# Three small layouts of a hybrid attention/mLSTM block: made by transfers in place of TensorE operations

## The reference

```python
def rmsnorm(x, g):
    y = x32 * lax.rsqrt(jnp.mean(x32 * x32, axis=-1, keepdims=True) + EPS)
    return (y * g.astype(jnp.float32)).astype(x.dtype)

# window_sink_attention: CHUNK = 64, a query chunk sees its own and the previous chunk
v_band = jnp.concatenate([shift_chunks(v, j) for j in (1, 0)], axis=2)      # 128 keys per query chunk
out = jnp.einsum('bnkgqs,bnskd->bnqkgd', probs, v_band)

# mlstm_chunkwise: state carried from chunk to chunk
m_new = jnp.maximum(f_l + m_st, m_l)
a = jnp.exp(f_l + m_st - m_new)
c_new = a[..., None, None] * c_st + e[..., None, None] * c_l
num = s_qk @ v + w_inter[..., None] * jnp.einsum('bhntk,bhnkv->bhntv', q, c_prev)

# reference
h = rmsnorm(x, norm1_g[l])
x = x + hybrid_mixer(h, w_in[l], ...)       # z = h @ w_in + b_in; attention | mLSTM; norms; @ w_out
h = rmsnorm(x, norm2_g[l])
x = x + conv_ffn(h, w_up[l], ...)           # 1024 -> 2*2816 -> 1024
return rmsnorm(x, final_g)
```

## Time and profile before

| what | value |
|---|---|
| median of 3 runs | 1001.22 us |
| profiled execution, its own time | 1000.0 us |
| its span, first to last instruction | 998.3 us |
| TensorE busy (matmuls) | 990.3 us, 99% |
| VectorE, ScalarE, GpSimd busy | 741.0, 508.1, 54.1 us |
| granted TensorE clock, mean | 0.999 |
| TensorE in the chain that ended last | 97% |

### The profile page before, as it was taken

The page is one execution under the profiler, slowest core; times in us unless marked ns, Lnnn a source line. Parts: engine busy times, 40 slices in busy tenths (PEclk is TensorE's granted clock), DMA queues, the critical chain, the costliest instruction groups (busy, mean ns, idle before and its releaser), DMA issues.

```text
span 998.3 us, 12909 instructions
## 1 busy us (share of the span) xinstructions
PE 990.3 (99%) x4725; PEld 812.0 (81%) x4725; DVE 741.0 (74%) x1155; ACT 508.1 (51%) x979; POOL 54.1 (5%) x53
## 2 busy tenths in 40 slices
PE   9999999999999999999999999999999999999997
PEld 7788887877888888888888888888888888888886
DVE  4573667866655669997777777777776879996796
ACT  5663556575633236754445445545445534444573
POOL 1000323311300000000000000000000000000000
PEclk9999999999999999999999999999999999999999
DMA  9528565223722242342232223223223999045104
GB/s 343 190 75 244 169 210 174 81 84 143 281 85 85 85 127 84 106 126 65 84 94 77 64 96 95 64 85 105 63 85 122 393 345 320 1 123 192 34 1 169
DMA packets 93256, 133.98 MB, mean 134 GB/s; under 512 B 5884, under 2 KB 56188, under 8 KB 93192
## 3 DMA queue, kind: packets, MB, share of 16 engines
q1 hardware_dynamic: 92664, 132.72, 39.9%
q10 hardware_dynamic: 432, 0.42, 0.1%
q0 software_dynamic: 96, 0.00, 0.1%
HBM read 104.75 MB, written 28.35 MB: 133 GB/s over the span
## 4 chain that ended last, share of the span: by engine, by line
PE 97%; DVE 1%; issue 1%; POOL 0%; ACT 0%; ACTq 0%; POOLq 0%
PE pz L2086 8%; PE pz L2369 8%; PE pz L2370 8%; PE pz L2371 8%; PE pd L2369 6%; PE pd L2370 6%; PE pd L2371 6%; PE pd L2393 4%; PE pd L2390 4%; PE pd L2392 4%; PE pz L2390 3%; PE pz L2393 3%; PE pz L2392 3%; PE pd L2272 3%; PE pd L2274 3%; PE pd L2273 3%
## 5 line engine op out<-in xcount | busy, mean ns | idle before, releaser
L1133 ACT ACTIVATE ws_hi<-raw 128x512 fp32r<-128x512 f32 x88 | 52.9, 626 | 102.8 <-PE pz L2371 47.3
L2369 PE MATMUL pz<-ht_hi,ws_hi 128*128 128x512 f32 x240 | 93.5, 390 | 0.0
L2371 PE MATMUL pz<-ht_hi,ws_lo 128*128 128x512 f32 x240 | 93.4, 389 | 0.0
L2370 PE MATMUL pz<-ht_lo,ws_hi 128*128 128x512 f32 x240 | 93.4, 389 | 0.0
L2369 PE MATMUL pd<-ht_hi,ws_hi 128*128 128x512 f32 x200 | 77.9, 389 | 0.0
L2371 PE MATMUL pd<-ht_hi,ws_lo 128*128 128x512 f32 x200 | 77.8, 389 | 0.0
L2370 PE MATMUL pd<-ht_lo,ws_hi 128*128 128x512 f32 x200 | 77.8, 389 | 0.0
L1836 DVE SCALAR_TENSOR_TENSOR gate<-u,vec,gate 128x1023 f32<-128x1023 f32 (+1 forms) x44 | 56.5, 1284 | 19.4 <-ACT gate L1175 18.6
L1806 DVE TENSOR_TENSOR ws_lo<-raw,ws_hi 128x512 fp32r<-128x512 f32 x88 | 58.6, 687 | 0.7 <-ACT ws_hi L1133 0.7
L1836 DVE SCALAR_TENSOR_TENSOR lift<-u,vec,lift 128x1023 f32<-128x1023 f32 (+1 forms) x44 | 56.3, 1279 | 0.1
L1208 ACT ACTIVATE d_hi<-a 128x512 fp32r<-128x512 f32 x44 | 27.7, 631 | 53.6 <-PE pd L2393 25.0
(11 more groups left out here) (311 smaller groups left out, 2562.9 us busy)
## 6 DMA issues: line engine op xcount, KB each, us to landing
raw<-in_w_up SPq DMA_DIRECT2D x48, 512.0 KB, 5.0
b<-in_w_down SPq DMA_DIRECT2D x49, 256.0 KB, 6.8
act_rows<-gate SPq DMA_DIRECT2D x22, 512.0 KB, 2.6
a<-act_rows SPq DMA_DIRECT2D x44, 256.0 KB, 4.6
w_raw<-in_w_wide SPq DMA_DIRECT2D x16, 512.0 KB, 3.4
x_turned<-in_x_t SPq DMA_DIRECT2D x8, 512.0 KB, 9.1
x_in<-in_x SPq DMA_DIRECT2D x8, 512.0 KB, 12.8
wo_hi_rows<-wo_new_hi SPq DMA_DIRECT2D x8, 512.0 KB, 5.1
```

Of the source, the lines that this page charges most:

```text
L1133: nc.scalar.activation(ws_hi[m][:, :, :], summand(p, i), ACT.Copy).then_inc(s["ws_hi_made"], 1)
L2369: mm(dst, wh[:, k, :], xh[:, k, :], start=begins and k == 0, stop=False, skip_group_check=not begins)
L2370: mm(dst, wh[:, k, :], xl[:, k, :], start=False, stop=False, skip_group_check=not begins)
L2371: ins = mm(dst, wl[:, k, :], xh[:, k, :], start=False, stop=k == KH - 1, skip_group_check=not begins)
```

## The change

Three things, all in the first 150 us of the program.

1. `x` is loaded in tiles of consecutive rows, so ScalarE's sums and the inverted roots come out as `rstd_tok` at once (token 128i + p at partition p, column i). SyncE stores that tile in order of tokens, now element by element: 1024 pieces of 4 bytes in place of 128 pieces of 32 bytes. The eight transposes and the copy are gone.
2. `carry` is filled by four transfers from the rows in memory, 64 x 8 elements of 4 bytes each, behind each head's `q_inter` in `spread_rows`. The two matmuls, `pair_rows` (a memset and a select on GpSimd) and the copy are gone; `rows_spread` counts 12 transfers, not 8.
3. `att_vb` is filled by two transfers that move the halves of `att_va`'s partitions, behind `load_tile(11)`. Seven transposes and two ScalarE copies are gone; `attend(2)` waits for the two transfers.

```diff
             def load_x(i):
-                sp.dma_start(x_in[:, i, :], x_d[i:S:NT, :]).then_inc(x_loaded[i // 4], 16)
+                sp.dma_start(x_in[:, i, :], x_d[i * P:(i + 1) * P, :]).then_inc(x_loaded[i // 4], 16)
...
             sp.wait_ge(s["x_rstd"], 1)
-            sp.dma_start(rstd_d.rearrange("(p i) -> p i", i=NT), rstd[:, :]).then_inc(s["rstd_stored"], 16)
+            sp.dma_start(rstd_d.rearrange("(i p) -> p i", p=P), rstd_tok[:, :],
+                         allow_slow_non_contiguous=True).then_inc(s["rstd_stored"], 16)
...
                     sp.dma_start(q_inter[(h % 2) * 64:(h % 2) * 64 + 64, h // 2, :],
                                  inter_d[h, :].partition_broadcast(64)).then_inc(s["rows_spread"], 16)
+                    sp.dma_start(carry[(h % 2) * 64:(h % 2) * 64 + 64, h // 2, :],
+                                 inter_d[h, P - 1:S:P].partition_broadcast(64),
+                                 allow_slow_non_contiguous=True).then_inc(s["rows_spread"], 16)
...
                 if n == 8:
                     spread_rows()
+                if n == 11:
+                    sp.wait_ge(s["att_v_made"], 1)
+                    for a in range(2):
+                        sp.dma_start(att_vb[a * CHUNK:(a + 1) * CHUNK, :, :],
+                                     att_va[(1 - a) * CHUNK:(2 - a) * CHUNK, a:a + NT - 1, :])\
+                          .then_inc(s["att_v_moved"], 16)
...
             def decay_keep(i):
                 if i == 0:
-                    pool.wait_ge(s["rows_spread"], 16 * 8)
+                    pool.wait_ge(s["rows_spread"], 16 * 12)
...
-                for c, dst in enumerate((att_va[:, 0:4, :], att_va[:, 4:8, :], att_vb[:, 0:4, :], att_vb[:, 4:7, :])):
+                for c, dst in enumerate((att_va[:, 0:4, :], att_va[:, 4:8, :])):
...
-            nc.vector.reciprocal(rstd[:, :], root[:, :]).then_inc(s["x_rstd"], 1)
+            nc.vector.reciprocal(rstd_tok[:, :], root[:, :]).then_inc(s["x_rstd"], 1)
...
-                dve.wait_ge(s["gates_turned"], 2)
-                nc.vector.tensor_copy(rstd_tok[:, :], bank[5][:, 2 * NT:3 * NT])
-                nc.vector.tensor_copy(carry[:, :, :], bank[5][:, 0:2 * NT].rearrange("p (r i) -> p r i", r=2))
+                dve.wait_ge(s["gates_turned"], 1)
...
             ins.then_inc(s["gates_turned"], 1)
-            pe.wait_ge(s["inter_made"], 1)
-            for r in range(2):
-                ins = mm(bank[5][:, r * NT:(r + 1) * NT], pair_rows[0:ML_HEADS, r, :], row_c[0:ML_HEADS, P - 1:S:P],
-                         start=True, stop=True)
-            pe.wait_ge(s["rstd_spread"], 16)
-            for i in range(NT):
-                ins = nc.tensor.transpose(bank[5][:, 2 * NT + i:2 * NT + i + 1], rstd_row[0:1, i * P:(i + 1) * P],
-                                          ident[0:1, 0:1])
-            ins.then_inc(s["gates_turned"], 1)
             z_block(7)
...
-                for n in range(2 * NT - 1):
-                    k0 = n * P if n < NT else CHUNK + (n - NT) * P
-                    ins = nc.tensor.transpose(bank[4 + n // 4][:, (n % 4) * P:(n % 4 + 1) * P], z[:, AV, k0:k0 + P],
-                                              ident[:, :])
+                for n in range(NT):
+                    ins = nc.tensor.transpose(bank[4 + n // 4][:, (n % 4) * P:(n % 4 + 1) * P],
+                                              z[:, AV, n * P:(n + 1) * P], ident[:, :])
...
                 c = n % 2 * 256
+                if n == 2:
+                    pe.wait_ge(s["att_v_moved"], 32)
```

More of the change, by code:

```diff
@@ L319, in hymba_kernel @@
         gate_w = at(40, "gate_w", [NK, 2 * ML_HEADS])
-        pair_rows = at(41, "pair_rows", [2, P])
         state = at(48, "state", [2, 2, ML_V + 1])
@@ L378, in hymba_kernel @@
             wo_hi_made wo_split
-            att_scored att_topped att_exped att_summed att_v_turned att_v_made
+            att_scored att_topped att_exped att_summed att_v_turned att_v_made att_v_moved
             att_p_turned att_p_made att_done att_kept att_squared att_sq_added att_p_scaled dve_step
@@ L760, in _ @@
             nc.gpsimd.memset(ones[:, :], 1.0).then_inc(s["mem_made"], 1)
-            nc.gpsimd.memset(pair_rows[0:ML_HEADS, :, :], 1.0).then_inc(s["mem_made"], 1)
             nc.gpsimd.memset(reset[:, :], 1.0).then_inc(s["mem_made"], 1)
@@ L769, in _ @@
             pool.dma_start(sinks[:, :], attn_sinks[0, :].partition_broadcast(P)).then_inc(s["small_loaded"], 16)
-            pool.wait_ge(s["mem_made"], 9)
+            pool.wait_ge(s["mem_made"], 8)
             nc.gpsimd.memset(reset[:, 0:S:P], 0.0).then_inc(s["const_made"], 1)
[L774 to L778, removed]
             pool.wait_ge(s["x_squared"], NT)
@@ L868, in z_keep @@
                 if b == 0:
-                    act.wait_ge(s["const_made"], 5)
+                    act.wait_ge(s["const_made"], 4)
                     act.wait_ge(s["small_loaded"], 48)
@@ L1439, in scale_q @@
                 dve.wait_ge(s["qk_made"], n + 1)
-                dve.wait_ge(s["rows_spread"], 16 * 8)
+                dve.wait_ge(s["rows_spread"], 16 * 12)
                 nc.vector.scalar_tensor_tensor(out=q_inter[:, n, :], in0=q_inter[:, n, :], scalar=ML_SCALE,
```

## The result

| | us |
|---|---|
| before, median (5 runs) | 1000.16 (999.31 to 1001.73) |
| changed, median (5 runs) | 1009.69 (1008.70 to 1011.24) |
| ratio (an estimate from all the runs) | 1.0094, 95% interval 1.0083 to 1.0105 |
| profiled execution, span | 1006.9, against 998.3 before |
| predicted | 999.5, range 998.0 to 1001.8 |

The removed TensorE work is gone, 1.78 us where 1.75 were forecast. Two stretches of waiting and a stretch at half the clock cost 10.8 us, six times as much. The profiled execution of the changed kernel (1008.70 us) is the quickest of the five, so what follows explains 8.6 us and not the 9.5 us between the medians. The kernel before has two runs more here than ahead of the prediction; its median moved from 1001.22 to 1000.16.

The account below looks back on a forecast made before the run. TensorE's own instruction list was taken to bound the kernel. Removed work of 1.03 + 0.72 = 1.75 us, with all transfers costing nothing, took the median from 1001.2 to 999.5 us, range 998.0 to 1001.8.

Parts of the forecast that it names:

- TensorE's work removed, 1.75 us: Matmuls and transposes gone ahead of block 7 (1.03 us) and at block 8 (0.72 us) shorten the run by their sum.
- I take 2.7, from the row with the same number of pieces: Factor store's extra time taken as 2.7 us, from a 1024-piece load landing in 4.1 us; it costs the run nothing.
- X: Extra time of the 1024-piece factor store; up to 5.5 us was said to pass before TensorE notices.
- The bound of 9.8 us: Extra time of the factor store if its whole 1.4 us grows with the number of pieces.
- Rival A: Factor store paid piece by piece; block 6 finds its inputs 4.3 us late, run 1003.8 us; chance 0.11.
- Block 5, "far more room": Block 5 needs only z_scale(1), so its cover against a late factor store was held not to be the limit.
- The carries, "nothing": Four carry transfers of 512 pieces take about 4 us of a full queue but cost the run nothing.
- D: Delay from the carry transfers to block 9's weights and the stores behind; may be 6.6 us without cost.
- whose next customer on TensorE stands in block 9, further off than those 6.6 us: ScalarE work moved by later stores and the load behind them has over 6.6 us of cover before TensorE needs it.
- The moves of the values, "nothing": Two half-megabyte value transfers behind block 11's weights have over 30 us of cover before first use and cost nothing.

Follow-up runs that it names:

- e4: Kernel before plus eight small test transfers behind its last store, each waiting for the one before, varying piece size, spacing and direction; its run time was not compared.
- e5: Changed kernel with 18 unused filler matmuls on TensorE between blocks 5 and 6, where it had waited: median 1010.48 us, ratio 1.0088.
- e12: Changed kernel with ScalarE's output-weight split moved behind the attention's exponentials, plus 18 filler matmuls before block 6: median 1003.65 us, ratio 1.0033.
- e2: Kernel before with only the carry edits (four transfers in place of two matmuls): median 1002.86 us, ratio 1.0019.
- e3: Kernel before with only the att_vb edits (two transfers in place of seven transposes): median 1001.57 us, ratio 1.0010.
- e11: Changed kernel with ScalarE's split of the output weights moved behind the attention's exponentials: median 1005.24 us, ratio 1.0054.
- e10: Kernel before with ScalarE's split of the output weights moved behind the attention's exponentials: median 1000.37 us, ratio 0.9997.

## Why the prediction was wrong

- **TensorE's work removed, 1.75 us: right.** The ledger has 1.02 and 0.76, and the earlier trace rows priced it by the starts.
- **"I take 2.7, from the row with the same number of pieces": the step that failed.** X was 11.4 - 1.4 = 10.0 us. The row matches in the number of pieces but is a load of 512-byte pieces; e4 shows that number and size alone cost about 1 us (2.6 against 1.4), and that packed writes to memory are a case of their own. The bound of 9.8 us was close by luck: it lets the time grow with the number of pieces, which would give 2.8 us for 256 packed pieces and 5.6 for 512, and e4 measured 7.4 and 4.4.
- **Rival A had the place and the size, and got 0.11.** Its sign came as written: a wait at line 2086 for VectorE before block 6, `z_scale(0)` at 53.86 and not before 49. Its reason, that the store is paid piece by piece, did not hold in e4. The read-modify-write below 512 bytes that the Trainium skill states ("DMA: Bandwidth & Descriptors", "Specifications") was set aside on the landing of 32-byte pieces in 1.4 us. As a price on every piece below 512 bytes it does not agree with e4 either: 4-byte pieces 512 bytes apart, each as far below 512 as the packed ones, land in 2.5 us. Rival A priced the waits at 4.3; they were 5.6. Block 5, "far more room", had 7.3 + 2.3 = 9.6 us and not the 10.0 needed; the store also went out 0.36 us later and TensorE came 0.3 us earlier (44.30 against 44.60), which makes most of the 1.4 us lost there.
- **The half clock was in no term.** A wait of 4.3 us cost 3.0 more in this execution. e5 and e12 show that it hangs on TensorE's idleness.
- **The carries, "nothing": wrong alone, 2.8 us in e2.** The range of D was sound, though the middle of 1.6 and 8.2 is 4.9 and not "about 4": the carries landed in 5.3 to 10.7 us, and block 9's weights in 11.3 rather than 9.4. What failed is "whose next customer on TensorE stands in block 9, further off than those 6.6 us". The cover behind the split was about 2 us, from the end of the exponentials at 107.7 to the scores at 109.85, and only 0.7 us by way of GpSimd. In e4 a store that landed 2.7 us later than in the earlier trace rows already made TensorE wait. I had followed the load to ScalarE and not on to what stands behind it in ScalarE's list.
- **The moves of the values, "nothing": right as transfers, and not enough.** They landed in 6.5 us at most, 30 us ahead of their use. But TensorE arriving 0.7 us earlier used up cover that hardly existed. That alone cannot cost more than the 0.7 us it gained; the rest of the loss in e3's profile is the store that landed late and the 1.6 us of half clock behind the wait. Whether this makes the whole of e3's median is not shown.

## What to carry to other kernels

When a layout is made by a transfer, look at which side the small pieces fall on: write memory in the order in which the data lie, and take the scattered side as a load, issued where the queue is empty and the data are needed late. Before counting a saving on a full engine, follow every transfer that gets later through the whole list behind its first user, down to the bottleneck's next wait; cover is the smallest gap on that way. Where a bottleneck waits for some microseconds, price the clock behind it too.

## What the runs showed of the hardware that I had not expected

- Packed 4-byte writes to memory: 10.3 us for 1024 of them in an empty queue (e4), 10.4 to 11.4 us in five other profiles, against 2.6 us for the same pieces 64 bytes apart, 2.1 us for the load and 2.4 us on chip.
- A single pause of TensorE of 4.3 us was followed by about 6 us at a granted clock of 0.51 in one execution, and by some 2.5 us in another of nearly the same kernel (e11). Two waits of 0.7 and 1.3 us in block 9 of the changed kernel were followed by no fall of the clock, two of 1.0 and 1.3 us at the same place in e3 by 3 us at 0.50.
- The same 512 KB store, issued at 78.2 to 78.3 us behind the same transfers, landed after 11.0 us in the kernel before, 13.0 in e10, 13.7 in e4 and 14.8 in e3. Where the split was not moved, this went with no wait in block 9, one of 0.4 us, and two of 1.0 and 1.3 us (e3 also reaches the place 0.8 us earlier).
